# Sums of weight blocks for five strips of seven-product tiles on GpSimd in place of VectorE

## The chip, the cores and the metric

The kernel runs on one core of a Trainium2 chip, in one launch. The metric is the time of one execution on the device, in microseconds (us). Everything is computed in 32-bit floating point.

## What is computed

The reference is two transformer-like blocks, one after the other, on 512 tokens of width 1024. Only the first mixer matters here. Cut to it:

```python
h = rms_norm(x, norm1_g)
z = h @ w_in
u_pool, u_lru, u_gate = z[..., :512], z[..., 512:1536], z[..., 1536:2560]
g_a = sigmoid(z[..., 2560:3584])
g_b = sigmoid(z[..., 3584:])
y_a = pooling_mixer(u_pool, pool_w, pool_scale) @ proj_a
y_b = rglru_mixer(u_lru, u_gate, ...) @ proj_b      # ends with: hidden states * gelu(u_gate)
x = x + (g_a * y_a + g_b * y_b) @ w_out
```

Behind it come a mixture of 16 experts, a second mixer and a second set of experts; their code is not touched.

## The kernel before

Every engine has a program of its own (`pe_front`, `dve_front`, `act_front`, `pool_front`, `sp_front` for the first mixer), written out in order by hand. The engines meet only through counting semaphores. `PE` is TensorE, `DV` VectorE, `AC` ScalarE, `PO` GpSimd and `SP` SyncE, which issues the weight loads (2048 KB each) into a ring of four buffers.

Six of the first mixer's products of a 1024x512 block of weights with the activations are made with seven products of quarter blocks in place of eight. A block of weights is a **strip** (`STRIPS`: g1, ga1, gb0, pb0, gb1, pb1, here called strip 0 to 5). A strip serves two **tiles**, so there are twelve tiles, p = 0 to 11, and strip b serves tiles 2b and 2b + 1. Per tile TensorE makes seven products (`sevenths`, L686); the first uses a raw block of the strip, and from the second on it needs the strip's sums: `PE.wait_ge(s_ws, 4 * (p // 2) + 4)`. The fifth product waits for ScalarE's first step of the tile (`act_first`, L579, through s_pa), and the sixth for VectorE's first step (L925, through s_pv).

The sums are made by `w_sum(b, i)`, i = 0 to 3, four per strip, each over 128 partitions by 1024 columns, taken as 4 runs of 256: z1, a new a21 written in place in the ring, z2, z4 (L908, L911, L914, L917). They start when the strip's weights have landed. The z blocks lie in `SETS[b]`; strips 3, 4 and 5 reuse the places of strips 1, 2 and 3, and so the first sum waits for `s_pp` at 14b - 14, the end of tiles 3, 5 and 7. In the kernel before VectorE makes them all: strip 0 long before tile 0, strip 1 between the merges of `dve_front` (L1051), and strips 2 to 5 inside `dve_pair`, two sums in each of tiles 1, 2, 4, 5, 6, 7, 8 and 9.

VectorE's work per tile is `dve_pair` (L925, L928, L931, L933, L938), five additions that read one operand from PSUM, and then, for some tiles, work on the result. Tiles 0 and 1: `gated` (L1037), a product of two SBUF tiles. Tiles 2 and 3: `merged` (L1042), one operand in PSUM. Tiles 6, 7, 10 and 11 (`PROJ`): twice L1069 (q = q * y) and L1072 (M = M + q), with both operands in SBUF; L1072 waits for the L1069 before it. After L1072 has run four times (s_m2 at 4), ScalarE may begin tile 8. Behind tile 3 VectorE also makes four sums of activations (`h_sums`, L892 to L897).

GpSimd's program in this stage is six small memsets at the start (`pool_front`). Its next work is `pool_few`, which gathers token rows for the experts, after the router.

SyncE's loads wait only for TensorE's counts (`sp_load`, L245). ScalarE's `act_pair` (L585) follows VectorE's L938.

Of the kernel before, what the change touches and what calls it, by code (L numbers as in the profile page):

```python
# [8 lines left out]
ALU = mybir.AluOpType  # L9
# [74 lines left out]
def build(nc, A, out):  # L84
    ctx = ExitStack()
    with ctx:
        PE, AC, DV, PO, SP = nc.tensor, nc.scalar, nc.vector, nc.gpsimd, nc.sync
# [5 lines left out]
        def sem(name):  # L93
            return ctx.enter_context(nc.semaphore(name))
# [57 lines left out]
        s_ga, s_ya, s_pp, s_o = sem("pe_ga"), sem("pe_ya"), sem("pe_sevenths"), sem("pe_o")  # L152
# [249 lines left out]
        s_bt, s_hid, s_gl, s_ybo = sem("dve_b"), sem("dve_hidden"), sem("act_gelu"), sem("dve_yb")  # L402
        s_gas, s_m, s_m2 = sem("act_ga"), sem("dve_ma"), sem("dve_mb")
        s_ht, s_ws, s_pa, s_pv = sem("dve_h_sums"), sem("dve_w_sums"), sem("act_sevenths"), sem("dve_sevenths")
# [270 lines left out]
        def strip(b):  # L675

            w, s, n = weights(STRIPS[b], 8)
            return [[w[:, 4 * i:4 * i + 4, 256 * j:256 * j + 256] for i in range(2)] for j in range(2)], s, n
# [193 lines left out]
        def pool_front():  # L872
            for b in UP + WP:
                PO.memset(b[:, 0:16], 0.0).then_inc(s_pl, 1)

        def dve_first_max(x, n, mx, oh, m2, prio):

# [18 lines left out]
            DV.wait_ge(s_ht, n + 3)  # L896
            DV.tensor_tensor(t4, b21, t2, ALU.subtract).then_inc(s_ht, 1)  # L897

        def w_sum(b, i):

            ((a11, a12), (a21, a22)), s, n = strip(b)
            z1, z2, z4 = SETS[b]
            if i == 0:
                DV.wait_ge(s, n)
                if b in (3, 4, 5):

                    DV.wait_ge(s_pp, 14 * b - 14)
                DV.tensor_tensor(z1, a21, a22, ALU.add).then_inc(s_ws, 1)  # L908
            elif i == 1:
                DV.wait_ge(s_ws, 4 * b + 1)  # L910
                DV.tensor_tensor(a21, a11, a21, ALU.subtract).then_inc(s_ws, 1)  # L911
            elif i == 2:
                DV.wait_ge(s_ws, 4 * b + 1)
                DV.tensor_tensor(z2, z1, a11, ALU.subtract).then_inc(s_ws, 1)  # L914
            else:
                DV.wait_ge(s_ws, 4 * b + 3)
                DV.tensor_tensor(z4, a12, z2, ALU.subtract).then_inc(s_ws, 1)  # L917

        def dve_pair(p, b, between):

            r1, r2, r3 = (bank[i] for i in st_banks(p))
            lo, hi, mid = st_tiles(p)
            DV.wait_ge(s_pp, 7 * p + 2)
            DV.wait_ge(s_pa, pa0(p) + 1)
            DV.tensor_tensor(hi[:, 256:512], lo[:, 0:256], r2[:, 0:256], ALU.add).then_inc(s_pv, 1)  # L925
            DV.wait_ge(s_pp, 7 * p + 4)
            DV.wait_ge(s_pv, 5 * p + 1)
            DV.tensor_tensor(mid, hi[:, 256:512].unsqueeze(1).to_broadcast([P, 2, 256]),  # L928
                             r3[:, :].rearrange("p (q t) -> p q t", q=2), ALU.add).then_inc(s_pv, 1)
            DV.wait_ge(s_pv, 5 * p + 2)  # L930
            DV.tensor_tensor(hi[:, 256:512], hi[:, 0:256], r3[:, 0:256], ALU.add).then_inc(s_pv, 1)  # L931
            DV.wait_ge(s_pp, 7 * p + 5)
            DV.tensor_tensor(lo[:, 0:256], lo[:, 0:256], r1[:, 256:512], ALU.add).then_inc(s_pv, 1)  # L933
            for i in between:
                w_sum(b, i)
            DV.wait_ge(s_pp, 7 * p + 7)
            DV.wait_ge(s_pv, 5 * p + 3)
            DV.tensor_tensor(mid, mid, r2[:, :].rearrange("p (q t) -> p q t", q=2), ALU.add).then_inc(s_pv, 1)  # L938

        def dve_front():  # L940
# [28 lines left out]
            for g in range(4):  # L969
                src, d, n = UP[g], 1, 0  # L970
                DV.wait_ge(s_up, g + 1)
                while d < 2 << g:
# [3 lines left out]
                    src, d, n = dst, 2 * d, n + 1  # L976
# [13 lines left out]
            for half in range(2):  # L990
                for j in range(4):
                    c = 4 * half + j
                    xc = XC[:, sl(j)]
                    DV.wait_ge(s_ul, c + 1)
                    if half:
                        DV.wait_ge(s_hid, c - 3)
                    DV.tensor_scalar(xc, Up[j][:, 0:512], p1("convw", 4 * c, 1), p1("convb", c, 1), ALU.mult, ALU.add)\
                        .then_inc(s_dv, dv())
                    for s in range(1, 3):
                        DV.wait_ge(s_dv, dv.n)  # L1000
                        DV.scalar_tensor_tensor(xc, Up[j][:, s:s + 512], p1("convw", 4 * c + s, 1), xc, ALU.mult, ALU.add)\
                            .then_inc(s_dv, dv())
                    DV.wait_ge(s_dv, dv.n)
                    DV.scalar_tensor_tensor(xc, Up[j][:, 3:515], p1("convw", 4 * c + 3, 1), xc, ALU.mult, ALU.add)\
                        .then_inc(s_xc, 1)
                if half:
                    DV.wait_ge(s_xc, 8)
                    h_sums(HT, ST1, 0)
                    for i in range(4):
                        w_sum(0, i)  # L1010
                for j in range(4):
                    c = 4 * half + j
                    inv = TM[j]
                    DV.wait_ge(s_th, c + 1)
                    DV.tensor_scalar(inv, T2[:, sl(j)], 1.0, None, ALU.add).then_inc(s_w1, 1)
                    DV.wait_ge(s_w1, c + 1)
                    DV.reciprocal(inv, inv).then_inc(s_dv, dv())
                    DV.wait_ge(s_sg, 2 * c + 2)
                    DV.wait_ge(s_xc, c + 1)
                    DV.tensor_tensor(I[:, sl(j)], I[:, sl(j)], XC[:, sl(j)], ALU.mult).then_inc(s_dv, dv())  # L1020
                    DV.wait_ge(s_dv, dv.n)
                    DV.wait_ge(s_ri, 2 * c + 2)
                    DV.tensor_scalar(XC[:, sl(j)], inv, 2.0, 1.0, ALU.mult, ALU.subtract).then_inc(s_dv, dv())
                    DV.wait_ge(s_rt, c + 1)
                    DV.tensor_tensor(T2[:, sl(j)], T2[:, sl(j)], inv, ALU.mult).then_inc(s_dv, dv())
                    DV.wait_ge(s_dv, dv.n)
                    DV.tensor_tensor(I[:, sl(j)], I[:, sl(j)], T2[:, sl(j)], ALU.mult).then_inc(s_bt, 1)
                if not half:
                    DV.wait_ge(s_yp, 4)
                for j in range(4):  # L1030
                    c = 4 * half + j
                    DV.wait_ge(s_bt, c + 1)
                    DV.tensor_tensor_scan(T2[:, sl(j)], XC[:, sl(j)], I[:, sl(j)], 0.0, ALU.mult, ALU.add).then_inc(s_dv, dv())
                    DV.wait_ge(s_dv, dv.n)
                    DV.tensor_copy(YB[:, sl(c)], T2[:, sl(j)]).then_inc(s_hid, 1)
# [10 lines left out]
                DV.wait_ge(s_gl, c + 1)  # L1046
                gated(c)
            for c in range(4):
                if c == 3:
                    for i in range(4):  # L1050
                        w_sum(1, i)  # L1051
                DV.wait_ge(s_gas, c + 2)
                merged(c, c)
            later = {1: (2, (0, 1)), 2: (2, (2, 3)), 4: (3, (0, 1)), 5: (3, (2, 3)), 6: (4, (0, 1)), 7: (4, (2, 3)),
                     8: (5, (0, 1)), 9: (5, (2, 3))}
            for p in range(12):
                dve_pair(p, *later.get(p, (0, ())))
                for i, (c, y) in enumerate(zip(reversed(st_cols(p)), (st_tiles(p)[1], st_tiles(p)[0]))):
                    if p < 2:
                        DV.wait_ge(s_pa, pa0(p) + 2 + i)  # L1060
                        gated(c)
                    elif p < 4:
                        DV.wait_ge(s_pa, pa0(p) + 2 + i)
                        merged(c, 2 * p + i)
                    elif p in PROJ:
                        q = TM[c % 4]
                        DV.wait_ge(s_pa, pa0(p - 2) + 2 + i)
                        DV.wait_ge(s_pv, 5 * p + 5)
                        DV.tensor_tensor(q, q, y, ALU.mult).then_inc(s_dv, dv())  # L1069
                        DV.wait_ge(s_dv, dv.n)  # L1070
                        DV.wait_ge(s_m, 8)
                        DV.tensor_tensor(M[:, sl(c)], M[:, sl(c)], q, ALU.add).then_inc(s_m2, 1)  # L1072
                if p == 3:

                    DV.wait_ge(s_ri, 16)
                    DV.wait_ge(s_yp, 4)
                    DV.wait_ge(s_pp, 14)
                    DV.wait_ge(s_ybo, 8)
                    h_sums(YB, STY, 4)
# [750 lines left out]
        for name in o_order:  # L1830
            i = int(name[1:])
# [391 lines left out]
        def dve_mixer2():  # L2223
# [61 lines left out]
            DV.wait_ge(k_x, 4)  # L2285
            h_sums(H2, ST2, 8)
            for i in range(4):
                w_sum(6, i)

            def merged(n):  # L2290

# [494 lines left out]
```

## Time and profile before

| | us |
|---|---|
| median of three runs | 2012.6 |
| lowest, highest | 2011.81, 2014.97 |
| span of the profiled execution, first to last instruction | 2008.8 |
| TensorE busy in the span | 1838.7 (92%) |
| VectorE busy | 594.7 (30%) |
| ScalarE busy | 284.9 (14%) |
| GpSimd busy | 33.8 (2%) |

The three runs gave the times; the profiled execution is known by its span alone, 3.8 us under the median. On the page, busy shares are averages over the whole span, and a line is a line of the kernel file. A row of the view in order of time gives the start in us from the span's start, the duration, the engine, the line, the operation and the tiles that it writes and reads (AR and ring are SBUF, ps is PSUM), how many instructions were merged into the row (x4), and in brackets how long the engine was idle before it and for whom. The seven-product tiles run from about 190 to 349 us. One quarter product appears as eight matmul instructions (1.73 us), a tile as 56.

### The profile page before, as it was taken

What the parts mean: (1) busy time and instruction counts of PE and PEld (TensorE: products, weight loads), DVE (VectorE), ACT (ScalarE), POOL (GpSimd) and SP (SyncE); (2) the same over time, 40 slices, a digit from 0 to 9 for tenths busy, and PEclk for the clock granted to TensorE, in tenths of its full rate; (3) what the DMA queues carried; (4) which work ended last, traced back from release to release, by engine and by line L of the source; (5) the groups of instructions that cost most, each with busy time, mean ns of one, the idle gap of its engine ahead of it and who ended that gap; (6) DMA issues with size and microseconds to landing.
All of it is one profiled execution on the core that took longest, in us unless ns stands there. A gap on an engine that the chain in (4) does not pass through costs nothing.

```text
span 2008.8 us, 20469 instructions
## 1 busy us (share of the span) xinstructions
PE 1838.7 (92%) x8840; PEld 842.9 (42%) x8840; DVE 594.7 (30%) x1109; ACT 284.9 (14%) x519; POOL 33.8 (2%) x44
## 2 busy tenths in 40 slices
PE   8999999999999989999998999888888888888886
PEld 4445788453333344567654333222222222222222
DVE  4478354341011245984323111111110111111112
ACT  3222100121101135131011000000000000000001
POOL 0000000010000010000000000000000000000000
PEclk9999999989999989999999999999999999999999
DMA  6221042369999952112458999999999999999996
GB/s 253 74 84 42 1 167 92 146 231 343 410 391 409 388 175 85 43 48 91 187 208 347 417 427 428 429 427 428 427 428 427 429 428 427 428 428 428 428 427 272
DMA packets 68544, 589.89 MB, mean 294 GB/s; under 512 B 5472, under 2 KB 6880, under 8 KB 37216
## 3 DMA queue, kind: packets, MB, share of 16 engines
q1 hardware_dynamic: 59904, 556.55, 67.3%
q10 hardware_dynamic: 4448, 17.28, 2.2%
q0 software_dynamic: 4096, 14.68, 2.1%
q8 instruction: 72, 1.18, 0.2%
q14 instruction: 24, 0.20, 0.0%
HBM read 575.91 MB, written 12.58 MB: 293 GB/s over the span
## 4 chain that ended last, share of the span: by engine, by line
PE 60%; DMA 33%; DVE 4%; issue 1%; ACT 1%; POOL 0%; ACTq 0%; DVEq 0%
PE ps L251 24%; DMA AR<-in_w_up 20%; PE ps L1287 11%; DMA AR<-in_w_down 11%; PE ps L2448 7%; PE ps L2474 5%; PE ps L829 3%; PE ps L2087 3%; DMA ring<-in_w_up 2%; PE ps L265 1%; PE ps L748 1%; PE ps L1982 1%; PE ps L2429 1%; PE ps L261 1%; DMA ring<-in_exp_w_gate 1%
## 5 line engine op out<-in xcount | busy, mean ns | idle before, releaser
L251 PE MATMUL ps<-AR,ring 128*128 128x512 f32 (+1 forms) x1160 | 384.5, 488 | 2.5 <-DVE AR L2278 2.4
L2588 DVE TENSOR_TENSOR XT<-XT,ps 128x512 f32<-128x512 f32 x128 | 82.0, 684 | 783.6 <-PE ps L2429 783.6
L251 PEld LDWEIGHTS ps<-AR,ring 128*128 128x128 f32 x1160 | 220.3, 190 | 157.3 <-issue 137.8
L2448 PE MATMUL ps<-ring,AR 128*64 128x512 f32 x1008 | 229.1, 597 | 47.7 <-DMA ring<-in_w_up 31.3
L2448 PE MATMUL ps<-AR 128*64 128x512 f32 x1040 | 235.8, 597 | 31.1 <-DMA AR<-in_w_up 25.2
L1287 PE MATMUL ps<-ring,AR 128*32 128x512 f32 x1536 | 249.5, 597 | 3.6 <-ACT AR L1436 2.2
L2448 PEld LDWEIGHTS ps<-ring,AR 128*64 128x64 f32 x1008 | 69.3, 136 | 199.9 <-issue 113.4
L2448 PEld LDWEIGHTS ps<-AR 128*64 128x64 f32 x1040 | 71.8, 136 | 191.5 <-issue 120.6
L251 PE MATMUL ps<-AR 128*128 128x256 f32 (+6 forms) x678 | 136.3, 346 | 7.1 <-DVE AR L1460 2.7
L1287 PE MATMUL ps<-AR 128*32 128x512 f32 x768 | 125.1, 595 | 0.0
L2474 PE MATMUL ps<-AR 128*64 128x512 f32 x528 | 117.9, 593 | 6.0 <-DMA AR<-in_w_down 6.0
L2474 PE MATMUL ps<-ring,AR 128*64 128x512 f32 x496 | 117.8, 623 | 4.4 <-ACT AR L2513 2.4
L251 PEld LDWEIGHTS ps<-AR 128*128 128x128 f32 (+2 forms) x678 | 107.9, 180 | 31.6 <-issue 13.1
L1287 PEld LDWEIGHTS ps<-ring,AR 128*32 128x32 f32 x1536 | 70.0, 110 | 100.1 <-issue 99.6
L265 PE MATMUL ps<-con,AR 128*128 128x128 f32 x360 | 62.6, 319 | 41.3 <-DVE AR L2602 31.0
L265 PEld LDWEIGHTS ps<-con,AR 128*128 128x128 f32 x360 | 51.7, 203 | 77.8 <-DVE AR L2602 44.3
L2508 ACT ACTIVATE AR<-ps 128x512 f32<-128x512 f32 x32 | 17.4, 594 | 441.7 <-PE ps L2448 441.7
L2474 PEld LDWEIGHTS ps<-AR 128*64 128x64 f32 x528 | 41.7, 137 | 79.1 <-issue 64.5
L2429 PE MATMUL ps<-AR 64*128 64x512 f32 x256 | 71.4, 638 | 0.7 <-issue 0.7
L2474 PEld LDWEIGHTS ps<-ring,AR 128*64 128x64 f32 x496 | 39.3, 144 | 71.4 <-issue 65.0
L1287 PEld LDWEIGHTS ps<-AR 128*32 128x32 f32 x768 | 33.6, 110 | 65.3 <-issue 64.8
L829 PE MATMUL ps<-ring,AR 128*128 128x512 f32 x128 | 57.5, 609 | 1.0 <-DVE AR L938 1.0
(373 smaller groups left out, 1225.9 us busy)
## 6 DMA issues: line engine op xcount, KB each, us to landing
AR<-in_w_gate SPq DMA_DIRECT2D x33, 2048.0 KB, 35.2
AR<-in_w_down SPq DMA_DIRECT2D x33, 2048.0 KB, 35.4
ring<-in_w_up SPq DMA_DIRECT2D x32, 2048.0 KB, 35.4
AR<-in_w_up SPq DMA_DIRECT2D x32, 2048.0 KB, 35.4
ring<-in_w_gate SPq DMA_DIRECT2D x31, 2048.0 KB, 32.1
ring<-in_w_down SPq DMA_DIRECT2D x31, 2048.0 KB, 35.4
ring<-in_w_in SPq DMA_DIRECT2D x15, 2048.0 KB, 8.9
ring<-in_exp_w_gate SPq DMA_DIRECT2D x15, 2048.0 KB, 9.0
```

Of the source, the lines that this page charges most:

```text
L251: x = PE.matmul(ps, l, r, start=i == 0, stop=i == len(pairs) - 1)
L261: PE.matmul(ps[:, 0:384], ident, con[:, 0:384], start=True, stop=True)
L265: x = PE.transpose(ps[:, sl(i, P)], s, ident)
L748: x = PE.matmul(bank[1 + g][:, :], w[:, k, g * P:g * P + P], HT[:, sl(k)], start=k == 0, stop=k == KT - 1)
L829: x = PE.matmul(bank[x_bank(i)][:, :], M[:, k * T + a * P:k * T + a * P + P], w[:, k, :], start=j == 0, stop=j == KT - 1)
L1287: yield k, c, PE.matmul(b[32 * c:32 * c + 32, :], rows(k), w(k), start=k == 0, stop=k == nk - 1, tile_position=(0, 32 * c), skip_group_che ...
L1982: x = PE.matmul(b[:, :], H2[:, k * T + a * P:k * T + a * P + P], wv[:, k, :], start=k == 0, stop=k == KT - 1)
L2087: x = PE.matmul(b[:, :], M2[:, k * T + a * P:k * T + a * P + P], w[:, k, :], start=j == 0, stop=j == KT - 1)
L2429: PE.matmul(co_bank(i)[:, :], cGE[b][r, a * P:(a + 1) * P], cYE[b][r, :], start=True, stop=True, tile_position=(64 * h, 0)).then_inc(e_co, 1)
L2448: x = PE.matmul(GU[2 * m + f // 2][64 * (f % 2):64 * (f % 2) + 64, :], XS[n // 2 % 2][:, k * P + 64 * b:k * P + 64 * b + 64], w[:, kk_, f ...
L2474: x = PE.matmul(DN[64 * h:64 * h + 64, :], cHB[b][:, k, :], w[:, kk_, h * 512:(h + 1) * 512], start=k == 0, stop=k == 15, tile_position=(0 ...
L2588: DV.tensor_tensor(XK[:, o:o + T], XK[:, o:o + T], co_bank(i)[:, :], ALU.add).then_inc(d_co, 1)
```

## The change

`w_sum` gets the engine as its first argument. VectorE keeps the sums of strip 0 (and of strip 6, in the second mixer). The twenty sums of strips 1 to 5 move to `pool_front`: GpSimd waits until the four sums of strip 0 are done (s_ws at 4) and until all hidden states are written (s_hid at 8, from where on the places of strips 1 and 2 are free), and then makes strip after strip with the same waits as before. VectorE's program loses them where they stood.

```diff
         def pool_front():
             for b in UP + WP:
                 PO.memset(b[:, 0:16], 0.0).then_inc(s_pl, 1)
+            PO.wait_ge(s_ws, 4)
+            PO.wait_ge(s_hid, 8)
+            for b in range(1, 6):
+                for i in range(4):
+                    w_sum(PO, b, i)
-        def w_sum(b, i):
+        def w_sum(E, b, i):
             ((a11, a12), (a21, a22)), s, n = strip(b)
             z1, z2, z4 = SETS[b]
             if i == 0:
-                DV.wait_ge(s, n)
+                E.wait_ge(s, n)
                 if b in (3, 4, 5):
-                    DV.wait_ge(s_pp, 14 * b - 14)
-                DV.tensor_tensor(z1, a21, a22, ALU.add).then_inc(s_ws, 1)
+                    E.wait_ge(s_pp, 14 * b - 14)
+                E.tensor_tensor(z1, a21, a22, ALU.add).then_inc(s_ws, 1)
...
-                w_sum(b, i)
+                w_sum(DV, b, i)
...
-                        w_sum(0, i)
+                        w_sum(DV, 0, i)
...
             for c in range(4):
-                if c == 3:
-                    for i in range(4):
-                        w_sum(1, i)
                 DV.wait_ge(s_gas, c + 2)
                 merged(c, c)
-            later = {1: (2, (0, 1)), 2: (2, (2, 3)), 4: (3, (0, 1)), 5: (3, (2, 3)), 6: (4, (0, 1)), 7: (4, (2, 3)),
-                     8: (5, (0, 1)), 9: (5, (2, 3))}
             for p in range(12):
-                dve_pair(p, *later.get(p, (0, ())))
+                dve_pair(p, 0, ())
```

The other three sums change in the same way, and `w_sum(6, i)` becomes `w_sum(DV, 6, i)`.

## Rows read from the trace of the kernel before

**Rows 1.** The page: span, and busy time, share and instructions of each engine.

```profile
span 2008.8 us, 20469 instructions
...
PE 1838.7 (92%) x8840; PEld 842.9 (42%) x8840; DVE 594.7 (30%) x1109; ACT 284.9 (14%) x519; POOL 33.8 (2%) x44
```

**Rows 2.** Chain of waits, 130 to 370 us: start us, us, what.

```profile
129.67 219.30 PE ps L251 x845
...
349.94 20.41 PE ps L829 x47
```

**Rows 3.** Waits of TensorE, 165 to 360 us: who for whom, us, times, longest.

```profile
PE ps L829 <- DVE AR L938: 1.0, 1, 1.0
```

**Rows 4.** VectorE by form: line, tiles, count; busy us, mean ns; idle.

```profile
L911 DVE TENSOR_TENSOR ring<-ring 128x1024 f32<-128x1024 f32 x6 | 7.4, 1225 | 0.2
```

**Rows 5.** GpSimd by form, the same columns.

```profile
L2620 POOL IOTA AR<- 128x512 f32 x1 | 0.6, 558 | 302.1 <-DVE AR L2538 302.1
...
L2186 POOL IOTA AR<- 128x128 f32 x1 | 0.2, 232 | 17.6 <-DVE XT L1516 17.6
```

**Rows 6.** VectorE in order of time: start us, us, what [idle before].

```profile
181.09 2.50 DVE L1037 TENSOR_TENSOR AR<-AR 128x512 f32<-128x512 f32 x4
...
193.67 0.42 DVE L925 TENSOR_TENSOR AR<-AR,ps 128x256 f32<-128x256 f32 x1 [2.69 <-PE ps L251]
...
289.35 0.69 DVE L1069 TENSOR_TENSOR AR<-AR 128x512 f32<-128x512 f32 x1
```

**Rows 7.** TensorE in order of time, the same columns.

```profile
195.20 5.34 PE L251 MATMUL ps<-AR,ring 128*128 128x256 f32 x24
...
215.92 3.62 PE L251 MATMUL ps<-AR 128*128 128x256 f32 x16
...
278.00 3.62 PE L251 MATMUL ps<-AR 128*128 128x256 f32 x16
...
302.17 3.62 PE L251 MATMUL ps<-AR 128*128 128x256 f32 x16
305.63 5.34 PE L251 MATMUL ps<-AR,ring 128*128 128x256 f32 x24
```

**Rows 8.** Loads in order of time; DMA issues: KB, us to landing.

```profile
252.71 0.58 SPq L245 DMA_DIRECT2D ring<-in_w_in  x1
...
253.33 3.24 SPq L245 DMA_DIRECT2D ring<-in_proj_b  x1
...
ring<-in_w_in SPq DMA_DIRECT2D x1, 2048.0 KB, 12.8
...
ring<-in_proj_b SPq DMA_DIRECT2D x1, 2048.0 KB, 17.5
```

**Rows 9.** All engines in order of time, 300 to 306 us.

```profile
300.65 0.69 DVE L938 TENSOR_TENSOR AR<-AR,ps 128x512 f32<-128x512 f32 x1 [0.64 <-PE ps L251]
301.44 0.69 DVE L1069 TENSOR_TENSOR AR<-AR 128x512 f32<-128x512 f32 x1
...
302.77 0.68 DVE L1069 TENSOR_TENSOR AR<-AR 128x512 f32<-128x512 f32 x1
303.49 0.69 DVE L1072 TENSOR_TENSOR AR<-AR 128x512 f32<-128x512 f32 x1
304.22 0.38 ACT L579 ACTIVATE AR<-ps 128x256 f32<-128x256 f32 x1 [13.49 <-DVE AR L1072]
```

**Rows 10.** All engines in order of time, around GpSimd's gathers.

```profile
438.62 1.15 DVE L1460 TENSOR_TENSOR AR<-con,AR 128x192 bf16<-128x192 f32 x4
...
438.91 1.69 POOL L1527 DMA_INDIRECT AR<-h_rows,AR  x1 [4.59 <-DVE AR L1469]
...
730.90 0.94 POOL L1534 DMA_INDIRECT AR<-y_rows,AR  x1 [0.30 <-issue]
...
733.84 1.28 DVE L1516 SCALAR_TENSOR_TENSOR XT<-AR,XT 128x1024 f32<-128x1024 f32 x1 [0.89 <-DMA AR<-y_rows,AR]
734.07 1.87 POOL L1534 DMA_INDIRECT AR<-y_rows,AR  x1 [0.30 <-issue]
```

More of the change, by code:

```diff
@@ L903, in w_sum @@
             if i == 0:
-                DV.wait_ge(s, n)
+                E.wait_ge(s, n)
                 if b in (3, 4, 5):
-                    DV.wait_ge(s_pp, 14 * b - 14)
-                DV.tensor_tensor(z1, a21, a22, ALU.add).then_inc(s_ws, 1)
+                    E.wait_ge(s_pp, 14 * b - 14)
+                E.tensor_tensor(z1, a21, a22, ALU.add).then_inc(s_ws, 1)
             elif i == 1:
-                DV.wait_ge(s_ws, 4 * b + 1)
-                DV.tensor_tensor(a21, a11, a21, ALU.subtract).then_inc(s_ws, 1)
+                E.wait_ge(s_ws, 4 * b + 1)
+                E.tensor_tensor(a21, a11, a21, ALU.subtract).then_inc(s_ws, 1)
             elif i == 2:
-                DV.wait_ge(s_ws, 4 * b + 1)
-                DV.tensor_tensor(z2, z1, a11, ALU.subtract).then_inc(s_ws, 1)
-            else:
-                DV.wait_ge(s_ws, 4 * b + 3)
-                DV.tensor_tensor(z4, a12, z2, ALU.subtract).then_inc(s_ws, 1)
+                E.wait_ge(s_ws, 4 * b + 1)
+                E.tensor_tensor(z2, z1, a11, ALU.subtract).then_inc(s_ws, 1)
+            else:
+                E.wait_ge(s_ws, 4 * b + 3)
+                E.tensor_tensor(z4, a12, z2, ALU.subtract).then_inc(s_ws, 1)
         def dve_pair(p, b, between):
@@ L2287, in dve_mixer2 @@
             for i in range(4):
-                w_sum(6, i)
+                w_sum(DV, 6, i)
             def merged(n):
```

## The prediction, made before the change was run

> **What bounds the kernel now.** I read the page first: TensorE is busy for 92% of the span, VectorE for 30%, GpSimd for 2% [rows 1]. That is an average over stages, so I read the chain of waits in the stretch that the change touches. It is one piece of TensorE work, 219.30 us long from 129.67 us, up to the output projection at 349.94 us; in between lies the last step of the last tile (L938) on VectorE [rows 2]. The waits of TensorE over the whole stage hold one entry, 1.0 us of the output projection for that same L938 [rows 3]. So within the twelve seven-product tiles TensorE waits for nobody: VectorE's work, the weight sums among it, is hidden. The change can then give back at most that 1.0 us, and it doesn't touch it: L938 of tile 11 adds the last product, which TensorE finishes just before, and the sums ended three tiles earlier. The question is what the change makes late.
>
> **The edit, part by part.**
>
> 1. What leaves VectorE: five strips of four sums, 20 instructions of 1.22 us [rows 4], 24.5 us. All lie beside matmuls, so this saves nothing at the end.
>
> 2. What GpSimd gets: the same 20 sums, each with two inputs in SBUF. The trace has no such instruction on GpSimd. The nearest rows are its two iotas: 232 ns for 128 columns and 558 ns for 512 [rows 5], hence 0.85 ns a column and 0.12 us fixed, for an instruction that only writes. A sum of 1024 columns reads two operands and writes one. If the reads go one after the other and the write beside them, it takes 0.12 + 2 x 0.87 = 1.86 us; if all three go one after another, 0.12 + 3 x 0.87 = 2.73 us. I take the middle, x = 2.3 us, and keep both ends. A strip is then 4 x 2.3 = 9.2 us (7.4 to 10.9).
> The Trainium skill has a price, in "GPSIMD Engine Reference", section 3.1: 4497 ns for an addition of 2048 columns. Halved, an estimate of 2.25 us; no row here shows it, and the sum below would come out 0.15 us smaller.
>
> 3. Are the sums in time? TensorE wants them at the second product of a strip's first tile; a tile is 12.1 us (two from 278.00 to 302.17 us).
> Strip 1 can start when the hidden states are done, at 181.09 us, where VectorE's gating starts on the same signal [rows 6], and is wanted at 215.92 us [rows 7]: 34.8 us for 9.2. Strip 2 follows it and is wanted more than two tiles later still.
> Strip 3 waits for its weights. Three loads were issued within 1.1 us; the second landed at 252.71 + 12.8 = 265.5 us, the third at 253.33 + 17.5 = 270.8 us [rows 8], 5.3 us apart, so the first at about 260.2 us. Sums end at 269.4 us, wanted at 278.00 us: 8.6 us spare, the tightest strip.
> Strips 4 and 5 wait for the tiles that still use their buffers: strip 5 for tile 7, which ends at 300.65 us, where L938 starts [rows 9], and strip 4 two tiles earlier, at 276.5 us. Each has 25.7 us for 9.2. Weights for both have landed by 270.8 us.
> So no sum is late up to 4.4 us apiece (17.8 us by four, strip 3). SP's and ACT's queues issue nothing new and wait for nothing new. On GpSimd's own queue the next work is the gather of token rows, which comes only behind the output projection at 349.94 us [rows 2], some 40 us after the last sum.
>
> 4. What runs beside the sums on VectorE. A seven-product step there has one input in PSUM; the gating (L1037), the merging (L1069, L1072) and the sums of activations have two in SBUF, as a GpSimd sum has. Does one hold up the other? The trace shows one direction. GpSimd's gather instruction, which reads indices, takes 0.94 us as a rule, but 1.87 us when it starts 0.23 us after VectorE's two-input L1516, which ran from 733.84 to 735.12 us: it ends 0.82 us after VectorE does [rows 10]. Beside four two-input L1460 back to back it took 1.69 us and ended 0.8 us after the fourth, so it got no turn between them. VectorE's rows there have their usual length, but a gather reads a few bytes; what a long GpSimd read does to VectorE no row shows. The bounds for each VectorE instruction with two SBUF inputs are 0 and x.
> The rule in the Trainium skill, "SBUF — State Buffer", section Who interferes with whom, speaks against the change: such an instruction and a reading GpSimd instruction exclude each other, and the second one waits for the whole of the first. The gather rows agree for the waiting of GpSimd; no run here yet shows VectorE waiting.
>
> 5. Where that would be paid. Go through the five windows.
> Strip 1 (181.1 to 190.3 us) meets the four gating steps. In the worst case each waits once, 9.2 us: gating ends at 192.8 us in place of 183.6. The three merges and one more (2.5 us) then end at 195.3 us and L925 of tile 0 at 195.7 us. In the trace L925 starts at 193.67 us [rows 6]; TensorE wants it at the sixth product, 195.20 + 3.45 = 198.65 us [rows 7]. Hidden, up to x = 3.0 us.
> Strip 2 ends at about the gating of tile 0, which nothing needs before tile 4, but L925 of tile 1 is queued behind it: one tile later than that of tile 0, 205.8 to 206.2 us, and wanted at 198.65 + 12.1 = 210.7 us. Two steps held cost 4.6 us against 4.5 us: hidden.
> Strip 3 (260 to 269 us) meets only steps with a PSUM operand. Strip 4 (276.5 to 285.7 us) ends before the merges of tile 6 at 289.35 us [rows 6].
> Strip 5 starts at 300.65 us, and 0.8 us later, at 301.44 us, VectorE comes to the four merging instructions of tile 7 [rows 9]. Here someone waits: ScalarE's first step of tile 8 needs the second merge, since it reuses buffers; it runs from 304.22 to 304.60 us, 0.05 us after L1072. TensorE wants it at the fifth product of tile 8, 305.63 + 1.73 = 307.36 us [rows 7]. Slack: 2.8 us.
> The first sum holds the first L1069 until 300.65 + x, a delay of x - 0.8. L1072 waits for L1069, so the second sum can go between: x more. The second L1069 follows the first L1072 without a gap (at 302.77 us); by the L1460 rows GpSimd gets no turn there. The last L1072 waits for that L1069, and the third sum goes between: x more. Delay 3x - 0.8, stall 3x - 0.8 - 2.8 = 3x - 3.6 = 3.3 us at x = 2.3 (2.0 to 4.6 at the ends of x). TensorE has no idle time afterwards to win it back [rows 2].
>
> **Sum.** Nothing saved, nothing late, 3.3 us of stall in tile 8. The profiled span goes from 2008.8 to 2012.1 us; the median of 2012.6 us lies 3.8 us over the span, so 2012.6 + 3.3 = 2015.9 us.
> The value between the ends 0 and 5.6 us (below) is the three turns, because the dependences in the code and the L1460 rows give three; that VectorE waits at all is the weaker step.
>
> **Rivals.**
> A. VectorE hardly waits: the shared access is only as short as in the gather rows, or at most two of the four merges are held. Stall 0, or 2x - 3.6 = 1.0 us. For it: VectorE's rows beside gathers aren't longer. Against: GpSimd did wait for the whole of VectorE's instruction. 2012.6 us (to 2013.6).
> B. GpSimd gets a turn before every merge: 4x - 3.6 = 5.6 us (3.8 to 7.3), 2018.2 us. For it: strict turns need only that a waiting engine goes first. Against: the four L1460. The change is then slower by a measurable amount, and it decides from 4x - 3.6 > 4.0, x over 1.9 us.
> C. The sums are far slower, by their rows of 256 columns or a fixed cost that the iotas don't show. From x = 3.0 us strip 1 stalls tile 0, from 4.4 us strip 3 stalls tile 6. At 4.5 us: 4 x 1.5 = 6 us in tile 0, 0.3 us in tile 6, and 4 x 4.5 - 3.6 = 14.4 us in tile 8 with four turns: some 21 us, 2033 us. Nothing in the profile speaks for so slow a GpSimd.
> D. Faster: only if L938 of tile 11 came earlier, and it waits for TensorE itself. A difference below zero would be scatter.
>
> **Chances.** A measurement of this kernel can tell about 0.2%, 4.0 us, from no change. Forecast, three turns: 0.35, of it 0.08 above 4.0 us (x over 2.53). A: 0.30. B: 0.26, nearly all above 4.0 us. C: 0.06. D: 0.03. Slower 0.08 + 0.25 + 0.06 = 0.39; same 0.27 + 0.30 + 0.01 = 0.58; faster 0.03. The range runs from A with the scatter of the three times of before (lowest 2011.8 us) to B at the upper end of x, 2012.6 + 7.4 = 2020.0 us; C stays outside.
>
> **What would show it.** In the profile after: twenty GpSimd sums of about 2.3 us, the last strip from about 300.7 us; L1069 and L1072 of tile 7 either later or drawn out, and the last one ending near 310 us (before: 304.2); a wait of TensorE for ScalarE's L579 of about 3.3 us near 307 us, the only new wait; everything before 300 us at its old place within 0.1 us. If L1072 ends at 304.2 us, A holds; at 312.6 us, B. A new wait of TensorE before a second product means that a sum was late (C). The prediction is wrong if VectorE gives way in another pattern, if a sum costs under 1.9 or over 2.7 us, or if the steps with one PSUM operand are held too.

## The result, and the profile after

| | before | after |
|---|---|---|
| median, us (4 runs each) | 2013.39 | 2022.13 |
| lowest, highest | 2011.81, 2014.97 | 2017.97, 2022.72 |
| span of the profiled execution | 2008.8 | 2016.7 |

The ratio is 1.004, 95% interval 1.0026 to 1.0053: the change makes the kernel slower, by 8.7 us of median and 7.9 us of span. The forecast was 2015.9 us, in a range up to 2020.0 us. The same program in a later comparison gave 2019.8 us against 2012.5 us. One execution of all those in this document, one of eleven in experiment 3, took 3863.15 us, which no trace explains, and its ratio leaves it out.

The chain of waits of the changed kernel from 290 to 380 us, in order of time (start us, us, what), which [rows 2] answers with a single piece of TensorE work. L930 to L943 are now the lines of `dve_pair`, L1042 is the gating, L913, L916, L919 and L922 are the sums, and L1069 and L1072 keep their numbers. "issue" is time in which the engine waits for nothing that the profile shows; the 2.50 us of it lie within the second merge's own row (304.72 to 307.44 us, below).

```profile
302.42 0.04 issue
302.46 2.23 DVE AR L1069
304.69 0.02 issue
304.72 0.04 DVE AR L1072
...
304.86 2.50 issue
307.36 2.84 DVE AR L1069
310.20 0.02 issue
310.22 2.72 DVE AR L1072
312.95 0.02 issue
312.97 0.39 ACT AR L579
...
313.41 43.41 PE ps L251 x192
```

All four merges of tile 7 stand in the chain, then ScalarE's first step of tile 8. The waits of TensorE from 165 to 370 us (who for whom, us, times, longest) have one entry more than [rows 3]:

```profile
PE ps L251 <- ACT AR L579: 4.9, 1, 4.9
PE ps L829 <- DVE AR L943: 1.0, 1, 1.0
```

The place itself, all engines in order of time, the answer to [rows 9]:

```profile
301.78 2.36 POOL L913 TENSOR_TENSOR AR<-ring 128x1024 f32<-128x1024 f32 x1 [14.63 <-PE ps L251]
302.46 2.22 DVE L1069 TENSOR_TENSOR AR<-AR 128x512 f32<-128x512 f32 x1
...
304.21 2.68 POOL L916 TENSOR_TENSOR ring<-ring 128x1024 f32<-128x1024 f32 x1
304.72 2.72 DVE L1072 TENSOR_TENSOR AR<-AR 128x512 f32<-128x512 f32 x1
...
306.85 2.79 POOL L919 TENSOR_TENSOR AR<-AR,ring 128x1024 f32<-128x1024 f32 x1
307.36 2.83 DVE L1069 TENSOR_TENSOR AR<-AR 128x512 f32<-128x512 f32 x1
309.72 2.67 POOL L922 TENSOR_TENSOR AR<-ring,AR 128x1024 f32<-128x1024 f32 x1
310.22 2.71 DVE L1072 TENSOR_TENSOR AR<-AR 128x512 f32<-128x512 f32 x1
```

Each merge took 0.69 us before and takes 2.22 to 2.83 us now. The records of both engines contain the time in which they were held: a merge begins while the GpSimd sum ahead of it still runs, and ends 0.54 us after that sum's row ends, less than its own 0.69 us; the next sum's row in turn begins about 0.5 us before the merge's row ends. Four sums, four merges, one after the other in turns. The last merge ends at 312.93 us, 7.7 us later than before when counted from the second product of tile 8 (303.19 us here, 302.17 us in [rows 7]).

TensorE's own rows show a second loss behind the wait:

```profile
303.19 3.62 PE L251 MATMUL ps<-AR 128*128 128x256 f32 x16
306.65 1.89 PE L251 MATMUL ps<-AR,ring 128*128 128x256 f32 x8
313.41 5.41 PE L251 MATMUL ps<-AR,ring 128*128 128x256 f32 x16 [4.87 <-ACT AR L579]
318.65 1.89 PE L251 MATMUL ps<-AR 128*128 128x256 f32 x8
```

The sixteen instructions from 313.41 us are the fifth and sixth product. Until the next product starts at 318.65 us they take 5.24 us, where two products take 3.45 us. The busy time by stretches shows why (us, then the busy time and instructions of PE, PEld, DVE, ACT and POOL, then the granted clock, DMA share and GB/s):

```profile
308.50:313.40 4.90, 0.04 (x1) 0.00 (x0) 4.40 (x2) 0.38 (x1) 3.81 (x2) 1.00 0.03 10
313.40:317.00 3.60, 3.59 (x9) 2.90 (x10) 1.57 (x4) 0.00 (x0) 0.00 (x0) 0.54 0.02 5
317.00:321.00 4.00, 4.00 (x19) 3.47 (x19) 0.81 (x2) 0.00 (x0) 0.00 (x0) 0.98 0.00 0
```

TensorE stands still for 4.9 us, and the granted clock is 0.54 in the 3.6 us after it: the lower of its two levels, 1.2 of 2.4 GHz, for nearly all of them.

A measure that is free of scatter between executions is the length of the **stage** from the second product of tile 8 to the first matmul of the output projection. Before: 302.17 to 349.94 us, 47.77 us. After: 303.19 to 357.78 us, 54.59 us. The difference of 6.82 us is 4.87 us of wait, 0.16 us before it (the fourth product ends at 308.54 us, while the fifth would have started at 306.65 + 1.73 = 308.38 us) and 5.24 - 3.45 = 1.79 us behind it. Behind the shorter waits of experiments 5 and 6, with the clock at full speed, that last term is 0.11 us (3.56 less 3.45). So 0.27 us belong to any such wait, and 1.7 us to the slow clock. Of the 7.9 us of span, 1.0 us more lies before the stage: the first product of the kernel (L748) starts at 20.43 us in place of 19.41 us. In the nine experiments below the stage begins anywhere from 301.92 to 304.89 us, though in none of them does TensorE wait between 165 us and tile 8; I take the 1.0 us as scatter. From the output projection to the end the two executions agree within 0.1 us (1658.92 and 1658.86 us). That closeness is chance: in the traces of the nine experiments this part takes 1657.9 to 1664.3 us, and the two with all or most sums on GpSimd and no wait in tile 8 (experiments 4 and 3) have 1657.9 and 1660.8 us. So single times scatter by some 6 us behind the stage, whatever the sums do.

### The profile page after: what moved, and what is told of

It is laid out like the page before. It is cut to its first block, busy times and chain, and to the rows that moved or that the text cites. A ratio compares the mean times of both kernels' runs of the same rounds, so it can differ in the third digit from the quotient of the medians.

```text
span 2016.7 us, 20470 instructions
## 1 busy us (share of the span) xinstructions
PE 1841.1 (91%) x8840; PEld 843.9 (42%) x8840; DVE 586.5 (29%) x1089; ACT 284.8 (14%) x519; POOL 83.2 (4%) x64
## 4 chain that ended last, share of the span: by engine, by line
PE 59%; DMA 34%; DVE 4%; issue 1%; ACT 1%; POOL 0%; ACTq 0%; DVEq 0%
PE ps L251 24%; DMA ring<-in_w_up 14%; PE ps L1287 11%; DMA AR<-in_w_up 9%; PE ps L2448 7%; DMA ring<-in_w_down 5%; PE ps L2474 5%; DMA AR<-in_w_down 4%; PE ps L2087 3%; PE ps L829 3%; PE ps L265 1%; PE ps L748 1%; PE ps L1982 1%; DMA ring<-in_exp_w_gate 1%; PE ps L2429 1%
## 5 line engine op out<-in xcount | busy, mean ns | idle before, releaser
L2448 PE MATMUL ps<-ring,AR 128*64 128x512 f32 x1008 | 229.3, 598 | 46.5 <-DMA ring<-in_w_up 30.7
L2474 PE MATMUL ps<-ring,AR 128*64 128x512 f32 x496 | 121.8, 640 | 5.9 <-DMA ring<-in_w_down 3.4
```

What stands on the lines that cost most here:

```text
L2448: x = PE.matmul(GU[2 * m + f // 2][64 * (f % 2):64 * (f % 2) + 64, :], XS[n // 2 % 2][:, k * P + 64 * b:k * P + 64 * b + 64], w[:, kk_, f ...
L2474: x = PE.matmul(DN[64 * h:64 * h + 64, :], cHB[b][:, k, :], w[:, kk_, h * 512:(h + 1) * 512], start=k == 0, stop=k == 15, tile_position=(0 ...
```

## Experiments

Theory T: the loss is made in tiles 7 and 8 alone, by VectorE and GpSimd taking turns. Rival R: the loss is spread over all sums. The ratio after is of times against the kernel before on the same chip.

**1. The changed kernel once more** (label e1_after_again, no edit).

> The changed kernel once more, for a second trace and more times. Theory T (the loss is made in tiles 7 and 8: the four merges of tile 7 take turns with the four sums of strip 5, TensorE stands still for 4.9 us and then runs for about 3.5 us at half its clock, 1.8 us more): the same wait of 4.9 us for ScalarE's L579 and the same stretch at a granted clock near 0.5, 6.8 us in all between the start of tile 8's second product and the output projection, and a time 0.3 to 0.45% over before. Rival R (the loss is spread: every GpSimd sum costs TensorE a little, by shared memory access, and tile 8 is only part of it): the wait is there too, but other stretches between 190 and 300 us or behind 360 us are longer than in before as well, by 2 us or more together.

Measured: 2019.82 us against 2012.54 us, ratio 1.0047 (1.0031 to 1.0063). The wait is 4.9 us again, and the stage is 303.49 to 358.07 us, 54.58 us. The granted clock behind the wait is 0.54. No other stretch of TensorE from 190 to 300 us waits, and the part behind the output projection, 1660.4 us, lies within the scatter named above. The loss repeats to 0.01 us in the stage; the median moves by more than that between comparisons (8.7 and 7.3 us), so the small terms are read from the stage below.

**2. Only strip 5 on GpSimd** (e2_only_strip5).

```diff
-            PO.wait_ge(s_ws, 4)
-            PO.wait_ge(s_hid, 8)
-            for b in range(1, 6):
-                for i in range(4):
-                    w_sum(PO, b, i)
+            PO.wait_ge(s_ws, 20)
+            for i in range(4):
+                w_sum(PO, 5, i)
...
             for c in range(4):
+                if c == 3:
+                    for i in range(4):
+                        w_sum(DV, 1, i)
                 DV.wait_ge(s_gas, c + 2)
                 merged(c, c)
             for p in range(12):
-                dve_pair(p, 0, ())
+                dve_pair(p, *{1: (2, (0, 1)), 2: (2, (2, 3)), 4: (3, (0, 1)), 5: (3, (2, 3)), 6: (4, (0, 1)), 7: (4, (2, 3))}.get(p, (0, ())))
```

> Only the four sums of strip 5 are GpSimd's; strips 1 to 4 go back to VectorE where they stood. Theory T: the whole loss stays, 6.8 us in tile 8 (4.9 us wait, 1.8 us at the low clock), time within 1 us of the changed kernel. Rival R: sixteen of twenty sums are gone from GpSimd, so at least half of the loss that doesn't stand as a wait in tile 8 goes with them, and the time falls by 1.5 us or more against the changed kernel.

Measured: 2019.57 us, ratio 1.0036 (1.0022 to 1.0049), against 2019.82 us of the changed kernel beside it. Wait 4.9 us; stage 303.75 to 359.07 us, 55.32 us, 0.7 us longer still, because the granted clock was low for longer. Busy time by stretches, the columns as above:

```profile
309.00:314.00 5.00, 0.10 (x2) 0.01 (x1) 4.48 (x2) 0.38 (x1) 3.89 (x2) 0.80 0.05 18
314.00:317.50 3.50, 3.50 (x8) 2.85 (x9) 1.53 (x3) 0.00 (x0) 0.00 (x0) 0.50 0.00 0
317.50:321.00 3.50, 3.50 (x14) 2.94 (x13) 0.42 (x1) 0.00 (x0) 0.00 (x0) 0.80 0.02 5
```

A mean of 0.80 is the lower level for two fifths of the stretch. So here the clock fell near 312.0 us, while TensorE was still standing, and came back near 318.9 us; the fifth and sixth product took 5.95 us, 2.4 us more than at full speed. Taking sixteen of the twenty sums away from GpSimd gives nothing back. R falls.

**3. Strips 1 to 4 on GpSimd, strip 5 on VectorE** (e3_strip5_on_vector).

```diff
-            for b in range(1, 6):
+            for b in range(1, 5):
...
-                dve_pair(p, 0, ())
+                dve_pair(p, *{8: (5, (0, 1)), 9: (5, (2, 3))}.get(p, (0, ())))
```

> GpSimd makes strips 1 to 4, VectorE strip 5 where it stood (tiles 8 and 9). Theory T: no wait of TensorE in tiles 0 to 11, the time of before within 0.1%. The gating of tile 0 still takes turns with strip 1 (8.9 us for four instructions in place of 2.5) and costs nothing. Rival R: sixteen of the twenty sums remain, so 1.5 to 2 us of the loss remain, 0.1% over before.

Measured: 2012.69 us, ratio 0.9999 (0.9990 to 1.0009); stage 304.89 to 352.66 us, 47.77 us, that of before to the last digit. The turns are there at strip 1 all the same. VectorE in order of time, of this run:

```profile
183.80 8.95 DVE L1042 TENSOR_TENSOR AR<-AR 128x512 f32<-128x512 f32 x4
192.68 2.47 DVE L1047 TENSOR_TENSOR AR<-AR,ps 128x512 f32<-128x512 f32 x4
```

The four gating steps took 2.50 us before [rows 6] and take 8.95 us, and nobody waits for them. The row under it is as telling: the four merges with one operand in PSUM take 0.62 us each beside a sum. (The fourth sum of strip 1 runs from 192.29 to 194.98 us.) The same collision is free at one place and costs 6.8 us at another.

**4. Strip 5 on GpSimd, but behind the merges** (e4_all_after_merges).

```diff
             for b in range(1, 6):
                 for i in range(4):
+                    if b == 5 and i == 0:
+                        PO.wait_ge(s_m2, 4)
                     w_sum(PO, b, i)
```

> As the changed kernel, but GpSimd waits before the first sum of strip 5 until the four merges of tile 7 are done (the count that ScalarE's first step of tile 8 waits for). Theory T: the sums run from about 305 to 315 us, TensorE wants them at 327 us; no wait, the merges take 0.69 us each, time of before within 0.1%. Rival R: all twenty sums are still on GpSimd, so 2 us stay. A third possibility, that VectorE's next steps (one operand in PSUM) are held by the sums when these come later: tile 8's L930 to L938 would take over 2 us each, and TensorE would wait in tile 8 or 9.

Measured: 2011.20 us, ratio 0.9998 (0.9988 to 1.0008); stage 303.67 to 351.43 us, 47.76 us. All engines in order of time:

```profile
304.99 0.69 DVE L1074 TENSOR_TENSOR AR<-AR 128x512 f32<-128x512 f32 x1
305.71 0.38 ACT L579 ACTIVATE AR<-ps 128x256 f32<-128x256 f32 x1 [13.49 <-DVE AR L1074]
305.76 2.35 POOL L915 TENSOR_TENSOR AR<-ring 128x1024 f32<-128x1024 f32 x1 [18.14 <-DVE AR L1074]
306.20 0.42 DVE L932 TENSOR_TENSOR AR<-AR,ps 128x256 f32<-128x256 f32 x1 [0.52 <-ACT AR L579]
...
308.19 2.35 POOL L918 TENSOR_TENSOR ring<-ring 128x1024 f32<-128x1024 f32 x1
309.05 0.69 DVE L935 TENSOR_TENSOR AR<-AR,ps 128x512 f32<-128x512 f32 x1 [2.43 <-PE ps L251]
```

A sum takes 2.35 us when nothing holds it. VectorE's steps of tile 8 (L932, L935), with one operand in PSUM, take their 0.42 and 0.69 us in the middle of it, so the third possibility falls too. All twenty sums are off VectorE and the time is that of before: the change costs nothing when strip 5 keeps clear of the merges, and it gains nothing either.

**5. Two sums ahead of the merges** (e5_two_sums_first): the edit of experiment 4 with `i == 2`.

> As the changed kernel, but only two of strip 5's four sums may run before the merges of tile 7 are done. Theory T (one turn for each sum that is ready): two merges are held, by 1.5 and 2.0 us, two take 0.69 us; delay 3.6 us less 2.8 us of slack, so TensorE waits 0.8 us in tile 8. If instead VectorE is slowed by sharing while GpSimd runs, in proportion to the overlap, all four merges are drawn out a little. Open is whether the clock falls behind so short a wait; if it does, tile 8 loses up to 1.8 us more.

**6. Three sums ahead** (e6_three_sums_first): with `i == 3`.

> Three of strip 5's sums may run before the merges of tile 7 are done. Theory T: three merges held, 1.5 + 2.0 + 2.1 = 5.6 us, less 2.8 us: TensorE waits 2.8 to 2.9 us. That is the case of the prediction (3.3 us), reached here by leaving the fourth sum out of the way. With the low clock behind it 4.6 us in all, without it 2.9 us.

Measured, one execution each (2013.69 and 2019.32 us, beside a kernel before that spread from 2008.5 to 2016.3 us, so only the stages are read):

| sums ready before the merges | merges, us | wait of TensorE | stage | over 47.77 us |
|---|---|---|---|---|
| 0 (experiment 4) | 0.69 0.69 0.68 0.69 | 0 | 47.76 | 0 |
| 2 | 2.22 2.72 0.68 0.69 | 0.70 | 48.73 | 0.96 |
| 3 | 2.22 2.72 2.83 0.69 | 2.84 | 50.90 | 3.13 |
| 4 (changed kernel) | 2.22 2.72 2.83 2.71 | 4.87 | 54.59 | 6.82 |

Each sum that is ready holds exactly one merge, also L1069 that follows L1072 without a gap. The first turn costs 1.53 us, the others 2.03, 2.14 and 2.02 us; less the slack of 2.8 us this gives 0.8, 2.9 and 4.9 us. Both losses with two and three sums are the wait and 0.27 us, within 0.02 us. The granted clock after the wait of 2.84 us, busy time by stretches of e6_three_sums_first:

```profile
308.10:311.00 2.90, 0.07 (x1) 0.00 (x0) 2.40 (x2) 0.38 (x1) 1.55 (x2) 1.00 0.06 20
311.00:314.60 3.60, 3.59 (x17) 3.18 (x18) 1.95 (x4) 0.00 (x0) 1.98 (x1) 1.00 0.02 5
```

It stays at 1.00, and the sixteen instructions take 3.72 us in place of 5.41 us. So the clock fell in the three traces with a wait of 4.9 us (the changed kernel, experiments 1 and 2) and not in the one with 2.84 us. How safe a wait of that length is, one trace doesn't show: in experiment 2 the clock fell about 2.9 us after TensorE had stopped (309.09 to 312.0 us).

**7. Work for TensorE in the wait** (e7_filler_products).

```diff
+            if p == 8:
+                idle_products(bank[0], 7)
             PE.wait_ge(s_pa, pa0(p) + 1)
             product(r1, 1, a12, b21)
```

> The changed kernel, with seven products that nobody reads, of 384 columns each, in TensorE's queue ahead of the fifth product of tile 8 (about 4.5 us of work, in the place of the 4.9 us of standing still). Nothing else changes; VectorE and GpSimd collide as before. If the clock falls because TensorE stands still, the granted clock stays at 1.00, the fifth and sixth products take 1.73 us each in place of 3.5 us and 1.8 us, and the loss between tile 8's start and the output projection is 5.0 us in place of 6.8 us. If the slow products have another cause (the collision, late weights), they stay slow, and the loss is 6.8 us or more.

Measured: 2017.97 us, ratio 1.0026 (1.0017 to 1.0036). TensorE in order of time:

```profile
308.08 4.68 PE L261 MATMUL ps<-con 128*128 128x384 f32 x14
313.12 3.72 PE L251 MATMUL ps<-AR,ring 128*128 128x256 f32 x16 [0.36 <-ACT AR L579]
```

and the busy time by stretches:

```profile
313.10:316.70 3.60, 3.58 (x17) 3.17 (x18) 1.95 (x4) 0.00 (x0) 0.00 (x0) 1.00 0.00 0
```

The collision is unchanged (merges of 2.22 to 2.83 us), the clock stays at 1.00, and the stage is 302.90 to 355.81 us, 52.91 us: 5.14 us over before in place of 6.82 us. Products that nobody reads take 1.7 us off the loss in this trace; the median, 5.1 us over that of before, agrees. That splits it: 5.1 us of waiting and starting again, 1.7 us of clock.

**8. Writes beside the merges** (e8_writes_beside_merges), and **9. copies** (e9_copies_beside_merges). The sums of strip 5 wait for the merges as in experiment 4; in their old place stand four memsets into the three z blocks that the sums will fill, or four copies of one weight block into them.

```diff
+                    if b == 5 and i == 0:
+                        PO.wait_ge(*strip(5)[1:])
+                        PO.wait_ge(s_pp, 56)
+                        for m in range(4):
+                            z = SETS[5][m % 3]
+                            if m > 2:
+                                PO.wait_ge(s_po, m - 2)
+                            PO.memset(z, 0.0).then_inc(s_po, 1)
+                        PO.wait_ge(s_po, 4)
+                        PO.wait_ge(s_m2, 4)
```

The copies have `PO.tensor_copy(z, strip(5)[0][1][0])` in place of the memset.

> The sums of strip 5 wait for the merges of tile 7; in their old place GpSimd makes four memsets of 128 by 1024 into the same blocks, which write and read nothing. If it is the reading of GpSimd that excludes a VectorE instruction with two SBUF inputs, the merges take 0.69 us each and TensorE waits for nobody. If GpSimd's writing holds VectorE too, each merge is held for a memset (about 1 us by the iotas), the last ends 3 us later, and TensorE waits up to 0.5 us.

> As the run with memsets, but GpSimd makes four copies of 128 by 1024 (one SBUF input, one output) beside the merges of tile 7, and the sums of strip 5 after them. If any reading on GpSimd excludes a VectorE instruction with two SBUF inputs, each merge is held for about the length of a copy (1 to 2 us): with 1 us the last merge ends about 3 us later and TensorE waits 0 to 0.5 us, with 2 us it waits some 4 us. If only GpSimd instructions with two inputs do that, the merges take 0.69 us each.

Measured, one execution each: 2016.54 us with memsets (before: 2008.52 to 2016.32 us) and 2015.51 us with copies (before: 2013.39 us, one execution); only the stages are read. In order of time, memsets first:

```profile
302.44 3.63 POOL L886 MEMSET AR<- 128x1024 f32 x4 [14.62 <-PE ps L251]
303.15 0.69 DVE L1079 TENSOR_TENSOR AR<-AR 128x512 f32<-128x512 f32 x1
...
303.87 0.69 DVE L1082 TENSOR_TENSOR AR<-AR 128x512 f32<-128x512 f32 x1
...
304.48 0.69 DVE L1079 TENSOR_TENSOR AR<-AR 128x512 f32<-128x512 f32 x1
305.20 0.69 DVE L1082 TENSOR_TENSOR AR<-AR 128x512 f32<-128x512 f32 x1
```

and the copies:

```profile
300.50 5.36 POOL L886 COPY AR<-ring 128x1024 f32<-128x1024 f32 x4 [14.65 <-PE ps L251]
301.19 0.90 DVE L1079 TENSOR_TENSOR AR<-AR 128x512 f32<-128x512 f32 x1
...
302.12 1.41 DVE L1082 TENSOR_TENSOR AR<-AR 128x512 f32<-128x512 f32 x1
303.45 1.52 DVE L1079 TENSOR_TENSOR AR<-AR 128x512 f32<-128x512 f32 x1
305.00 1.41 DVE L1082 TENSOR_TENSOR AR<-AR 128x512 f32<-128x512 f32 x1
```

Beside memsets a merge keeps its 0.69 us. Beside copies it is held, for 0.2 to 0.8 us: one operand read holds VectorE for less than half of what two do (2.0 us). The last merge then ends 2.5 us later, inside the slack, and both stages are 47.77 us. So GpSimd holds a VectorE instruction with two SBUF operands only when it reads, and for longer when it reads two operands. That it is VectorE's second SBUF operand that is shut out is concluded from the steps with one operand in PSUM, which nothing held.

No version here beats the kernel before: TensorE doesn't wait for VectorE in this stage, so there was nothing to win, and the 1.0 us ahead of the output projection (0.98 to 1.01 us) is the same in all runs.

## Why the prediction was wrong, point by point

- **Bound, and nothing saved** (first part and point 1): right. With strip 5 clear of the merges (experiment 4) 24.5 us of VectorE's work are gone and the ratio is 0.9998 (0.9988 to 1.0008).
- **Price of a sum** (point 2): 2.35 us against 2.3 us, which was the middle between two guesses at how the reads and the write overlap; that it came so close is in part luck. Right for the question whether the sums are in time; too large for the turns. A turn costs VectorE 2.02 to 2.14 us: about 0.3 us of a sum doesn't hold it. Here the mechanism was right and the size a little too large. The estimate of 2.25 us from the Trainium skill's price ("GPSIMD Engine Reference", section 3.1) lies 0.1 us under the row.
- **Sums in time** (point 3): right. The tightest strip, strip 3, ran from 261.32 to 270.83 us and was wanted at 279.02 us. One reading was wrong and cost nothing: strip 2 didn't follow strip 1. GpSimd waited 3.60 us for its weights, and its sums ran from 196.88 to 206.42 us.
- **What holds what** (point 4): that VectorE waits for GpSimd at all, the step called the weaker one, was right. The Trainium skill's rule ("SBUF — State Buffer", Who interferes with whom) agrees with every run on who holds whom: two SBUF operands against a reading sum or copy are held, one operand in PSUM isn't, and memsets hold nobody. On the length the rows differ from it a little: a merge is held for 2.0 to 2.1 us of a sum's 2.35 us, not for the whole.
- **Where it is paid** (point 5): right, to the tile, the instruction and the waiting engines; strips 1 to 4 cost nothing, as worked out. Strip 2 did hold a gating step of tile 0 (two took 2.87 us in place of 1.30 us), and it stayed hidden. The sign that everything before 300 us would keep its place within 0.1 us failed: all came 1.0 us later, by the scatter before 21 us.
- **Three turns** (point 5): this is the first step that failed: GpSimd took four turns and not three. From the gather beside four L1460 I took it that GpSimd gets no turn between VectorE instructions that follow without a gap. It does: L1069 was held directly behind L1072, and the four gating steps, which don't wait for one another, took 8.96 us. The fourth turn is the whole difference between the waits for 3 and 4 sums in the table: 2.03 us. Experiment 6 leaves that turn out and waits 2.84 us, where the prediction had 3.3 us. A sum that is waiting goes ahead of a VectorE instruction that comes later. Why the gather got no turn is open; no run was made for it.
- **The clock** (not in the prediction): the second failed step. I priced the wait at its own length. Standing still for 4.9 us made the granted clock fall to half, which cost 1.7 us more (experiment 7; 2.4 us in the trace of experiment 2), and the sum and the range had it at nothing. The general rule of the Trainium skill ("TensorE: Matmul & The Clock Gate", Part 1) that the clock falls back when TensorE is idle and comes back once it works again agrees with this; I didn't weigh it.
- **Sum**: rival B had 5.6 us and the runs show 4.9 us of wait; with the 0.27 us of starting up and 1.7 us of clock it is 6.8 us, so 2012.6 + 6.8 = 2019.4 us, inside the range, and 1.2 us above the value for B. That B comes so near is in part luck: its turns are 0.7 us too dear, and 1.95 us behind the wait are missing. The first four runs had a median of 2022.1 us, 1.3 times as far from before as the stage alone explains; the comparison of experiment 1 gave 7.3 us. The three runs beside which the forecast was made had a median of 2012.6 us, and with the fourth it is 2013.4 us: 6.8 us on top of that is already 2020.2 us. I take the remaining 1.9 us as scatter, which the traces show at over 6 us behind the output projection, and for which I had left too little room at the upper end; it is not traced, since the profiled execution (2017.97 us) is the lowest of the four.

## What to carry to other kernels

A GpSimd instruction that reads SBUF isn't free beside VectorE: list the VectorE instructions with two SBUF operands in its window, charge each one a full turn, and ask for each who waits for it and with how much slack. Here five windows held three collisions, two free and one worth 6.8 us, and one wait in GpSimd's program separates them. If the stall comes to several microseconds, add what TensorE's clock takes to recover (1.7 and 2.4 us here).

## What the runs showed of the hardware

- The records of both engines include the time for which they are held: a merge of 0.69 us reads up to 2.83 us, a sum of 2.35 us reads 2.79 us. Busy time goes up though no work was added.
- GpSimd's sums and VectorE's instructions with two SBUF operands alternated one for one in both places where both had several ready (the gating steps and the merges of tile 7): 2.64 to 2.87 us from sum to sum, 0.69 us of merge and about 2.0 us of sum.
- TensorE's granted clock stayed at 1.00 over a wait of 2.84 us and fell to 0.54 behind one of 4.87 us. In one execution (experiment 2) it fell before the wait of 4.90 us was over and stayed at the lower level until about 4.9 us behind it, which cost another 0.7 us.
